# Attention values with the queries on the partitions, row sums applied after the values, and heads turned in pairs

## The chip, the core and the metric

The kernel runs on one core of a Trainium2 chip, as one launch. The metric is the time of the whole launch on the device, in microseconds (us). TensorE multiplies matrices: a weight load puts the stationary operand (up to 128x128) into the array, and a matmul streams the moving operand past it, one output row of up to 512 elements per partition, into PSUM. ScalarE (ACT), VectorE (DVE) and GpSimd (POOL) do the elementwise work, SyncE (SP) issues the transfers. The engines run side by side and wait for each other through semaphores. PE stands for TensorE's matmuls and PEld for its weight loads.

## The reference

An encoder of two layers over 512 tokens of width 1024. Each layer has an attention part with 16 heads of three kinds, an output projection, a residual with layer norm, and an MLP. The heads are 4 of kind A (a mixture of three dilated windows with a shared position bias, which the kernel folds into one softmax with a bias band), 4 of kind B (low-rank q and kv, 96 wide keys) and 8 of kind C (grouped queries on 2 key/value heads). What matters here is the core that all kinds share:

```python
def blocked_attention(q, k, v, scale):
    ...
        s = jnp.einsum('bhgqd,bhkd->bhgqk', qblk, k, preferred_element_type=jnp.float32) * scale
        p = jax.nn.softmax(s, axis=-1)
        return jnp.einsum('bhgqk,bhkd->bhgqd', p.astype(v.dtype), v)
    ...
    y = jnp.concatenate([heads_to_seq(y_a), heads_to_seq(y_b), heads_to_seq(y_c)], -1) @ w_o[l]
    x = layer_norm(ALPHA * x + (1.0 + g_a) * y, ln1_g[l], ln1_b[l])
```

Each value v is 64 wide per head, and there are 512 keys and 512 queries.

## The kernel before

Every matrix product is done in three matmuls on a split of each float32 operand into a high part of type fp32r and a low part (helper `three`, lines 1503 to 1507: high x high, high x low, low x high). ACT makes the high parts (Copy into an fp32r tile) and DVE the low ones (a subtraction).

A layer goes through the input projections, the attention, the output projection in two column halves (`wo0`, `wo1`), and eight MLP groups. Each engine has its own hand-written order for all of it, and the attention is a software pipeline over 64 units (16 heads in the order C, A, B, with 4 tiles of 128 queries each). In step s the engines do this, each in this order:

- PE (lines 1713 to 1741): the scores of unit s (stationary q of 128 queries, moving k of 512 keys, two matmuls for heads C and A, where the second half of the rows holds the low part of q, and three for B) into bank s % 3; four transposes (line 1722) of the probabilities of unit s-3 into one bank of three; and half of the values of two units. For the values the stationary operand is v (128 keys x 64) and the moving one the transposed probabilities of two units, 128 keys x 256 queries, so the output has 64 partitions (the value's elements) and 256 queries. A step has 6 of these matmuls, a head 24.
- DVE (lines 1150 to 1195): the row maximum of unit s (L1165, for heads A with the band added, L1161), the low part `pt_lo` of the transposed probabilities of unit s-4 (L1178), once per head the low part of a finished head's output (L1186, 64 partitions x 512), and the low parts of the next heads' q (L1146), k (L1139) and v (L1194).
- ACT (lines 806 to 844): Exp of unit s with the row sum (L813), the high part `pt_hi` of unit s-3 (L822), once per head the high part of a head's output (L832), and the high parts of the next q, k and v (L797, L792, L841).
- POOL (lines 529 to 542): for each unit the reciprocal of the 128 row sums (L535, a power of -1) and the scaling of the 128x512 probabilities by it (L536). In the second layer DVE takes the reciprocal for units 8 to 23 (L1172), and POOL puts behind each of these scalings one part of the layer norm's gain and shift on X (L487, L490).

PE's transposes wait for POOL's scaling (`normed`), PE's values for `pt_lo` (`pt_ready`). After the last unit PE waits for all of the low parts of the heads' output (`y_ready`), and then starts `wo0`. The heads' output goes into `hT_hi` and `hT_lo`, where the normalised activations stood before.

## Time and profile before

| | |
|---|---|
| time, median of 3 runs | 1406.24 us (1404.43 to 1406.99) |
| the profiled execution's own time | 1406.55 us |
| its span, first to last instruction | 1404.7 us |
| busy: PE, PEld, DVE, ACT, POOL | 94%, 80%, 70%, 43%, 24% |
| attention of layer 1 (l = 0): first score to first matmul of wo0 | 185.29 to 311.61 us |
| attention of layer 2 (l = 1) | 858.33 to 989.98 us |
| granted TensorE clock, mean | 0.984 of 2.4 GHz |

The busy share of PE is not a share of its peak: matmuls overlap in the trace, and what a matmul costs in a stream is the distance from its start to the next one's start. Layers are called first and second below. In a form such as `bank<-pt_hi,v_hi 128*64 128x256` the first tile is the moving operand and the second the stationary one; 128*64 is the stationary operand's shape, 128x256 the moving one's.

### The profile page before, as it was taken

To read this page: it belongs to the slowest core of one execution; us is meant where nothing else is said; L and a number is where in the kernel's file an instruction comes from. 1 tells how busy PE (TensorE), PEld (TensorE's weight loads), DVE (VectorE), ACT (ScalarE), POOL (GpSimd) and SP (SyncE) were. 2 spreads that over 40 slices of the span, in tenths; PEclk is the share of its full clock that TensorE was granted. 3 is DMA by queue.
4 is the path that set the end of the run, shared out by engine and by line. 5 is a ranking of instruction groups with operands and counts; after the bars stand their busy time and mean duration, and the time that the engine had idled before them with its cause. 6 is when DMAs were issued, how large, how long until landed. Compare 5 with 4: busy or idle time off the path is not lost.

```text
span 1404.7 us, 19902 instructions
## 1 busy us (share of the span) xinstructions
PE 1315.9 (94%) x6888; PEld 1118.5 (80%) x6888; DVE 989.6 (70%) x1676; ACT 606.0 (43%) x1260; POOL 332.1 (24%) x427
## 2 busy tenths in 40 slices
PE   4998989899999999999999899889999999999995
PEld 2888777788988888888879878678788888888884
DVE  6668789975688665755775887999377954545577
ACT  0446479871632223222254546789253222222321
POOL 0013056650324000000030404967040700000005
PEclk9999999999999999999999998999999999999998
DMA  8864500003344443442246462000225433333322
GB/s 289 301 205 147 191 27 1 28 3 111 103 151 154 155 153 95 157 156 91 83 120 235 135 217 86 1 28 1 90 68 180 154 94 98 98 97 96 98 93 95
DMA packets 88165, 164.54 MB, mean 117 GB/s; under 512 B 8024, under 2 KB 18648, under 8 KB 88080
## 3 DMA queue, kind: packets, MB, share of 16 engines
q1 hardware_dynamic: 87408, 161.08, 35.2%
q10 hardware_dynamic: 672, 2.36, 0.5%
q8 instruction: 50, 0.82, 0.2%
q14 instruction: 35, 0.29, 0.1%
HBM read 159.21 MB, written 4.19 MB: 116 GB/s over the span
## 4 chain that ended last, share of the span: by engine, by line
PE 65%; DVE 13%; DMA 7%; ACT 6%; POOL 4%; issue 3%; SPq 0%; POOLq 0%; ACTq 0%; DVEq 0%
PE bank L1505 21%; PE bank L1506 20%; PE bank L1507 20%; DMA slab_raw<-in_w_in 5%; DVE ada_sum L938 2%; PE bank L1722 2%; DVE pt_lo L1178 2%; DMA ada_w<-in_w_ada 1%; DVE smax L1165 1%; ACT slab_hi L606 1%; PE bank L1536 1%; POOL prob L536 1%; DVE q_hi L1146 1%; DVE stats L1218 1%; ACT pt_hi L822 1%
## 5 line engine op out<-in xcount | busy, mean ns | idle before, releaser
L1505 PE MATMUL bank<-hT_hi,slab_hi 128*128 128x512 f32 (+1 forms) x640 | 235.9, 369 | 2.4 <-ACT kB L755 2.4
L1506 PE MATMUL bank<-hT_lo,slab_hi 128*128 128x512 f32 (+1 forms) x640 | 235.4, 368 | 0.0
L1507 PE MATMUL bank<-hT_hi,slab_lo 128*128 128x512 f32 (+1 forms) x640 | 235.4, 368 | 0.0
L1280 DVE TENSOR_TENSOR slab_lo<-slab_raw,slab_hi 128x512 fp32r<-128x512 f32 x240 | 172.3, 769 | 66.9 <-ACT slab_hi L880 44.3
L1505 PE MATMUL bank<-slab_hi,h_hi 128*128 128x512 f32 x512 | 201.5, 394 | 0.3 <-DVE slab_lo L1280 0.3
L1507 PE MATMUL bank<-slab_hi,h_lo 128*128 128x512 f32 x512 | 199.3, 389 | 0.0
L1506 PE MATMUL bank<-slab_lo,h_hi 128*128 128x512 f32 x512 | 199.3, 389 | 0.0
L1505 PE MATMUL bank<-slab_hi,hT_hi 128*128 128x384 f32 (+3 forms) x448 | 153.8, 343 | 10.5 <-DVE slab_lo L982 4.0
L982 DVE TENSOR_TENSOR slab_lo<-slab_raw,slab_hi 128x512 fp32r<-128x512 f32 (+3 forms) x144 | 83.2, 586 | 106.2 <-ACT slab_hi L606 106.0
L498 POOL TENSOR_SCALAR mv<-mv 128x1 f32<-128x1 f32 x16 | 5.5, 345 | 642.3 <-DVE mv L1226 641.6
L1506 PE MATMUL bank<-slab_lo,hT_hi 128*128 128x384 f32 (+3 forms) x448 | 151.2, 338 | 0.0
L1507 PE MATMUL bank<-slab_hi,hT_lo 128*128 128x384 f32 (+3 forms) x448 | 151.1, 337 | 0.0
L1505 PEld LDWEIGHTS bank<-hT_hi,slab_hi 128*128 128x128 f32 x640 | 120.7, 189 | 24.0 <-ACT kB L755 4.1
L1506 PEld LDWEIGHTS bank<-hT_lo,slab_hi 128*128 128x128 f32 x640 | 120.7, 189 | 20.0
L1507 PEld LDWEIGHTS bank<-hT_hi,slab_lo 128*128 128x128 f32 x640 | 120.7, 189 | 19.9
L938 DVE SCALAR_TENSOR_TENSOR ada_sum<-ada_w,c_col,ada_sum 128x512 f32<-128x512 f32 x168 | 127.7, 760 | 12.1 <-DMA ada_w<-in_w_ada 8.2
L606 ACT ACTIVATE slab_hi<-slab_raw 128x512 fp32r<-128x512 f32 (+3 forms) x144 | 74.2, 546 | 134.9 <-DMA slab_raw<-in_w_o 73.0
L1505 PEld LDWEIGHTS bank<-slab_hi,h_hi 128*128 128x128 f32 x512 | 96.1, 188 | 21.5 <-issue 1.9
L1506 PEld LDWEIGHTS bank<-slab_lo,h_hi 128*128 128x128 f32 x512 | 96.1, 188 | 20.7 <-issue 1.0
L1507 PEld LDWEIGHTS bank<-slab_hi,h_lo 128*128 128x128 f32 x512 | 96.1, 188 | 20.1
L1313 DVE TENSOR_TENSOR acc<-bank,acc 128x512 f32<-128x512 f32 x96 | 59.6, 682 | 72.8 <-PE bank L1507 72.8
L535 POOL TENSOR_TENSOR smax<-smax,mone 128x1 f32<-128x1 f32 x112 | 70.7, 631 | 149.7 <-ACT prob L813 149.5
(199 smaller groups left out, 2565.2 us busy)
## 6 DMA issues: line engine op xcount, KB each, us to landing
slab_raw<-in_w SPq DMA_DIRECT2D x256, 256.0 KB, 2.7
ada_w<-in_w_ada SPq DMA_DIRECT2D x48, 1024.0 KB, 6.1
slab_raw<-in_w_in SPq DMA_DIRECT2D x48, 192.0 KB, 5.1
slab_raw<-in_w_o SPq DMA_DIRECT2D x32, 256.0 KB, 2.7
slab_raw<-in_w_in SPq DMA_DIRECT2D x16, 256.0 KB, 4.2
band<-bias_rows SPq DMA_DIRECT2D x8, 448.0 KB, 3.2
slab_raw<-in_w_in SPq DMA_DIRECT2D x16, 144.0 KB, 4.7
X<-in_x SPq DMA_DIRECT2D x1, 2048.0 KB, 9.6
```

What stands on the lines that cost most here:

```text
L535: after(step(pool.tensor_tensor(smax[:, u % 4, 2:3], smax[:, u % 4, 1:2], mone[:, 0:1], ALU.pow)))
L536: pool.tensor_scalar(p, p, smax[:, u % 4, 2:3], 1.0, ALU.mult, ALU.mult).then_inc(normed, 1)
L606: act.activation(slab_hi[:, slot, 0:width], slab_raw[:, slot, 0:width], ACT.Copy).then_inc(slab_hi_done, 1)
L938: return dve.scalar_tensor_tensor(out=dst, in0=ada_w[:, k // 4, k % 4, :], scalar=c_col[:, 1, k:k + 1], in1=ada_b[:, :] if k == 0 else dst ...
L982: dve.tensor_tensor(slab_lo[:, slot, 0:width], slab_raw[:, slot, 0:width], f32(slab_hi[:, slot, 0:width]), ALU.subtract).then_inc(slab_lo_ ...
L1178: dve.tensor_tensor(pt_lo[:, half % 2, :, cols], t_bank(u)[:, :].rearrange("p (k q) -> p k q", k=TT), f32(pt_hi[:, half % 2, :, cols]), AL ...
L1280: dve.tensor_tensor(slab_lo[:, slot, :], slab_raw[:, slot, :], f32(slab_hi[:, slot, :]), ALU.subtract).then_inc(slab_lo_done, 1)
L1313: dve.tensor_tensor(dst, set_[t][:, :], dst, ALU.add).then_inc(evac_dve, 1)
L1505: pe.matmul(dst, a_hi, w_hi, start=first, stop=False)
L1506: pe.matmul(dst, a_hi, w_lo, start=False, stop=False)
L1507: return pe.matmul(dst, a_lo, w_hi, start=False, stop=last)
L1722: ins = pe.transpose(t_bank(u)[:, k * P:(k + 1) * P], prob[:, u % 4, k * P:(k + 1) * P], ident[:, :])
```

## The change

The probabilities are no longer scaled. They are transposed as Exp leaves them, and in the values' product the operands change places: the transposed probabilities of one unit (128 keys x 128 queries) are the stationary operand and v (128 keys x 64) is the moving one. The output then has the queries on the partitions: 128 x 64 for each unit, 4 units side by side in one bank. When a head's four units are done, DVE multiplies its 128 x 256 output by the reciprocals of the row sums, which POOL has made for the whole head in one instruction of 4 columns. For each pair of heads PE transposes the scaled output back (4 transposes of 128x128), ACT and DVE make the high and the low part in one 128 x 512 instruction each.

The pipeline gets shorter lags (transposes 2 steps behind, low part 3, values 4). POOL's gain and shift in the second layer are spread over heads 1 to 6. For heads A the low part of k is made once in place of twice, and the second score matmul uses its 64 rows alone. The last pair's turn lies inside wo0, which starts with the parts that are ready.

```diff
-T_LAG, LO_LAG, PV_LAG = 3, 4, 6
-ATT_STEPS = UNITS + 8
-AFFINE_FROM = 8
+PAIRS = NH // 2
+T_LAG, LO_LAG, PV_LAG = 2, 3, 4
+Y_LAG = 8 + PV_LAG + 1
+ATT_STEPS = UNITS + Y_LAG - 8 + 2
+AFFINE_IN = {1: 3, 2: 3, 3: 3, 4: 3, 5: 2, 6: 2}
...
-        pt_hi = over("pt_hi", [P, 2, TT, 256], 65536, F32R)
-        pt_lo = over("pt_lo", [P, 2, TT, 256], 73728, F32R)
+        pt_hi = over("pt_hi", [P, 4, TT, P], 65536, F32R)
+        pt_lo = over("pt_lo", [P, 4, TT, P], 73728, F32R)
```

In GpSimd's program:

```diff
-                for u in range(UNITS):
-                    p = prob[:, u % 4, :]
-                    if affine_unit(l, u):
-                        pool.wait_ge(summed, sums_by_dve(l, u) + 1)
-                    else:
-                        pool.wait_ge(exped, l * UNITS + u + 1)
-                        after(step(pool.tensor_tensor(smax[:, u % 4, 2:3], smax[:, u % 4, 1:2], mone[:, 0:1], ALU.pow)))
-                    pool.tensor_scalar(p, p, smax[:, u % 4, 2:3], 1.0, ALU.mult, ALU.mult).then_inc(normed, 1)
+                def reciprocals(i):
+                    pool.wait_ge(exped, l * UNITS + 4 * i + 4)
+                    if i >= 2:
+                        pool.wait_ge(y_scaled, l * NH + i - 1)
+                    pool.tensor_tensor(rsum(i), sums(i), mone[:, 0:TT], ALU.pow).then_inc(recip_done, 1)
+                    pool.wait_ge(recip_done, l * NH + i + 1)
```

In ScalarE's:

```diff
-                        act.activation(hT_hi[64 * hf:64 * hf + 64, kt, :], bank[5 + j % 2][0:64, :], ACT.Copy
-                                       ).then_inc(y_hi_done, 1)
+                    p, off = divmod(s - Y_LAG, 8)
+                    if off == 0 and p >= 0:
+                        act.wait_ge(y_turned, l * PAIRS + p + 1)
...
+                        act.activation(hT_hi[:, kt, :], t_bank(("Y", p))[:, :], ACT.Copy).then_inc(y_hi_done, 1)
```

In VectorE's:

```diff
-                        dve.reciprocal(smax[:, u % 4, 2:3], smax[:, u % 4, 1:2]).then_inc(summed, 1)
...
+                    i, off = divmod(s - PV_LAG - TT, TT)
+                    if off == 0 and 0 <= i < NH:
+                        dve.wait_ge(pv_done, l * UNITS + 4 * i + 4)
+                        dve.wait_ge(recip_done, l * NH + i + 1)
+                        dve.tensor_tensor(y_sb(i // 2)[:, :, 64 * (i % 2):64 * (i % 2) + 64],
+                                          bank[5 + i % 2][:, 0:256].rearrange("p (t d) -> p t d", t=TT),
+                                          rsum(i).unsqueeze(2).broadcast_to([P, TT, HD]), ALU.mult
+                                          ).then_inc(y_scaled, 1)
+                    p, off = divmod(s - Y_LAG - 1, 8)
+                    if off == 0 and p >= 0:
+                        dve.wait_ge(y_hi_done, l * PAIRS + p + 1)
...
+                        dve.tensor_tensor(hT_lo[:, kt, :], t_bank(("Y", p))[:, :], f32(hT_hi[:, kt, :]),
+                                          ALU.subtract).then_inc(y_ready, 1)
```

In TensorE's:

```diff
-                        dst = bank[5 + i % 2][0:64, (half % 2) * 256:(half % 2) * 256 + 256]
-                        vs, ps = KV[i] % 2, half % 2
-                        for k in (2 * odd, 2 * odd + 1):
-                            ins = three(dst, v_hi[:, vs, k, :], v_lo[:, vs, k, :], pt_hi[:, ps, k, :], pt_lo[:, ps, k, :],
-                                        k == 0, k == TT - 1)
-                pe.wait_ge(y_ready, l * NH + NH)
-                chunk_job("wo0", WO0, 512)
+                def turn_prob(u):
+                    pe.wait_ge(exped, l * UNITS + u + 1)
+                    turn_bank_free(("P", u))
+                    for k in range(TT):
+                        ins = pe.transpose(t_bank(("P", u))[:, k * P:(k + 1) * P], prob[:, u % 4, k * P:(k + 1) * P],
+                                           ident[:, :])
+                    ins.then_inc(transposed, 1)
+                def turn_y(p):
+                    pe.wait_ge(y_scaled, l * NH + 2 * p + 2)
+                    turn_bank_free(("Y", p))
+                    for t in range(TT):
+                        ins = pe.transpose(t_bank(("Y", p))[:, t * P:(t + 1) * P], y_sb(p)[:, t, :], ident[:, :])
+                    ins.then_inc(y_turned, 1)
+                def values(u):
+                    i, qt = divmod(u, TT)
+                    pe.wait_ge(pt_ready, l * UNITS + u + 1)
+                    if qt == 0:
+                        pe.wait_ge(v_ready, l * NKV + KV[i] + 1)
+                        if i >= 2:
+                            pe.wait_ge(y_scaled, l * NH + i - 1)
+                    dst, vs = bank[5 + i % 2][:, 64 * qt:64 * qt + 64], KV[i] % 2
+                    for k in range(TT):
+                        ins = three(dst, pt_hi[:, u % 4, k, :], pt_lo[:, u % 4, k, :], v_hi[:, vs, k, :],
+                                    v_lo[:, vs, k, :], k == 0, k == TT - 1)
+                    ins.then_inc(pv_done, 1)
+                for s in range(UNITS + PV_LAG):
+                    if s < UNITS:
+                        score(s)
+                    if 0 <= s - T_LAG < UNITS:
+                        turn_prob(s - T_LAG)
+                    p, off = divmod(s - Y_LAG, 8)
+                    if off == 0 and p >= 0:
+                        turn_y(p)
+                    if 0 <= s - PV_LAG:
+                        values(s - PV_LAG)
```

The new `wo_first` does what `chunk_job("wo0", ...)` did, with `turn_y` of the last pair before its second slab, a wait for that pair's low part before its last slab, and a wait for the last head's scaling before its third token tile.

## Rows read from the trace of the kernel before

**Rows 1.** The page's first part: busy us (share of span), count, by engine.
```profile
PE 1315.9 (94%) x6888; PEld 1118.5 (80%) x6888; DVE 989.6 (70%) x1676; ACT 606.0 (43%) x1260; POOL 332.1 (24%) x427
```

**Rows 2.** Both attentions: us; busy of PE, PEld, DVE, ACT, POOL; clock, DMA share, GB/s.
```profile
185.29:311.40 126.11, 113.01 (x784) 96.59 (x784) 114.35 (x199) 107.90 (x247) 84.73 (x128) 0.99 0.03 9
858.33:989.70 131.37, 118.86 (x784) 100.91 (x784) 119.19 (x215) 108.26 (x247) 98.08 (x128) 0.94 0.03 8
```

**Rows 3.** PE's waits in the first attention: total us, times, longest us.
```profile
PE bank L1505 <- DVE pt_lo L1178: 9.0, 6, 2.2
PE bank L1722 <- POOL prob L536: 2.0, 4, 1.2
```

**Rows 4.** Timeline of PE, a unit of a C head: start us, duration us.
```profile
213.20 0.40 PE L1709 MATMUL bank<-k_hi,q_hi 128*128 128x512 f32 x1
...
213.66 0.60 PE L1722 MATMUL bank<-ident,prob 128*128 128x128 f32 x4
214.02 0.36 PE L1505 MATMUL bank<-pt_hi,v_hi 128*64 128x256 f32 x1
...
214.80 0.40 PE L1709 MATMUL bank<-k_hi,q_hi 128*128 128x512 f32 x1
```

**Rows 5.** The same for a unit of a B head, and its successor's start.
```profile
285.69 0.40 PE L1505 MATMUL bank<-k_hi,q_hi 96*128 96x512 f32 x1
...
287.52 0.40 PE L1505 MATMUL bank<-k_hi,q_hi 96*128 96x512 f32 x1
```

**Rows 6.** Timeline of PE in a projection: 128-wide weights, 256 moving columns.
```profile
136.16 0.28 PE L1505 MATMUL bank<-slab_hi,hT_hi 128*128 128x256 f32 x1
136.28 0.28 PE L1506 MATMUL bank<-slab_lo,hT_hi 128*128 128x256 f32 x1
```

**Rows 7.** Timeline of PE in the MLP: eight loads of 128 weights, one moving column each.
```profile
593.53 0.94 PE L1477 MATMUL bank<-ones,ada_sum 128*128 128x1 f32 x8
594.33 0.49 PE L1505 MATMUL bank<-slab_hi,h_hi 128*128 128x512 f32 x1
594.66 0.40 PE L1506 MATMUL bank<-slab_lo,h_hi 128*128 128x512 f32 x1
```

**Rows 8.** One line's and one tile's instructions: duration ns min/median/max.
```profile
L1477 PEld LDWEIGHTS bank<-ones,ada_sum x128: 187/192/338, 15.1 to 857.6; 128*128 128x128 f32 x128
L1505 PEld LDWEIGHTS bank<-pt_hi,v_hi x256: 132/134/231, 194.6 to 988.0; 128*64 128x64 f32 x128
```

**Rows 9.** Weight loads by form, whole span: busy us, mean ns.
```profile
L1505 PEld LDWEIGHTS bank<-hT_hi,slab_hi 128*128 128x128 f32 x640 | 120.7, 189 | 24.0 <-ACT kB L755 4.1
```

**Rows 10.** DVE's groups in the first attention: busy us, mean ns, idle before.
```profile
L1178 DVE TENSOR_TENSOR pt_lo<-bank,pt_hi 128x512 fp32r<-128x512 f32 x64 | 43.6, 684 | 2.3 <-ACT pt_hi L822 1.1
L1186 DVE TENSOR_TENSOR hT_lo<-bank,hT_hi 64x512 fp32r<-64x512 f32 x16 | 10.9, 679 | 1.9 <-ACT hT_hi L832 1.7
L1139 DVE TENSOR_TENSOR k_lo<-qkA,k_hi 64x512 fp32r<-64x512 f32 x8 | 5.5, 687 | 1.7 <-ACT k_hi L792 1.5
L1194 DVE TENSOR_TENSOR v_lo<-vA,v_hi 128x256 fp32r<-128x256 f32 x4 | 1.7, 417 | 0.1
```

**Rows 11.** POOL's scalings in the second attention: busy us, mean ns.
```profile
L536 POOL TENSOR_SCALAR prob<-prob,smax 128x512 f32<-128x512 f32 x64 | 46.7, 729 | 5.5 <-DVE smax L1172 0.8
```

**Rows 12.** Timeline of PE, end of the first attention: idle us before, its releaser.
```profile
311.61 0.50 PE L1505 MATMUL bank<-slab_hi,hT_hi 128*128 128x512 f32 x1 [1.40 <-DVE hT_lo L1186]
```

**Rows 13.** Windows of 1 us, granted clock in the third column from the end.
```profile
188.00:189.00 1.00, 0.90 (x3) 0.30 (x2) 0.28 (x2) 0.95 (x4) 0.71 (x2) 0.90 0.00 0
867.00:868.00 1.00, 1.00 (x7) 0.87 (x6) 1.00 (x2) 1.00 (x3) 0.90 (x3) 0.77 0.00 0
925.00:926.00 1.00, 1.00 (x7) 0.94 (x6) 0.97 (x2) 0.48 (x1) 0.83 (x2) 0.74 0.00 0
```

**Rows 14.** Timeline of PE ahead of the last of those windows.
```profile
924.80 0.33 PE L1505 MATMUL bank<-pt_hi,v_hi 128*64 128x256 f32 x1 [1.84 <-DVE pt_lo L1178]
```

**Rows 15.** The chain that ended last, a stretch at half clock: start us, us.
```profile
41.54 1.88 PE bank L1477 x8
```

More of the change, by code:

```diff
@@ L81, with turns @@
 UNITS = NH * TT
-T_LAG, LO_LAG, PV_LAG = 3, 4, 6
-ATT_STEPS = UNITS + 8
-AFFINE_FROM = 8
-def affine_unit(l, u):
-    return l > 0 and AFFINE_FROM <= u < AFFINE_FROM + 4 * TT
-def sums_by_dve(l, u):
-    return sum(affine_unit(m, v) for m in range(l) for v in range(UNITS)) + sum(affine_unit(l, v) for v in range(u))
+PAIRS = NH // 2
[3 more added lines that the diff above has]
+AFFINE_IN = {1: 3, 2: 3, 3: 3, 4: 3, 5: 2, 6: 2}
+def turns():
+    out = []
+    for s in range(ATT_STEPS):
+        if 0 <= s - T_LAG < UNITS:
+            out.append(("P", s - T_LAG))
+        if s >= Y_LAG and (s - Y_LAG) % 8 == 0:
+            out.append(("Y", (s - Y_LAG) // 8))
+    return out
+TURNS = turns()
+TURN = {job: n for n, job in enumerate(TURNS)}
 OUT_AT = [(4 + h // 2, h % 2) if m == "C" else (h // 2, h % 2) if m == "A" else (2 + h // 2, h % 2)
@@ L528, in _ @@
                     pool.sem_inc(x_ready, TT)
-                for u in range(UNITS):
-                    p = prob[:, u % 4, :]
-                    if affine_unit(l, u):
-                        pool.wait_ge(summed, sums_by_dve(l, u) + 1)
-                    else:
-                        pool.wait_ge(exped, l * UNITS + u + 1)
-                        after(step(pool.tensor_tensor(smax[:, u % 4, 2:3], smax[:, u % 4, 1:2], mone[:, 0:1], ALU.pow)))
-                    pool.tensor_scalar(p, p, smax[:, u % 4, 2:3], 1.0, ALU.mult, ALU.mult).then_inc(normed, 1)
-                    if l > 0 and u == AFFINE_FROM:
-                        pool.wait_ge(bank_ready, l * B_LAYER + 16)
-                        pool.wait_ge(lnx_in, 32)
-                    if affine_unit(l, u):
-                        n = u - AFFINE_FROM
-                        affine_part(n // 4, n % 4, lnx_g, lnx_b)
+                def reciprocals(i):
[4 more added lines that the diff above has]
+                    pool.wait_ge(recip_done, l * NH + i + 1)
+                part = 0
+                for i in range(NH):
+                    if i >= 1:
+                        reciprocals(i - 1)
+                    for _ in range(AFFINE_IN.get(i, 0) if l > 0 else 0):
+                        if part == 0:
+                            pool.wait_ge(bank_ready, l * B_LAYER + 16)
+                            pool.wait_ge(lnx_in, 32)
+                        affine_part(part // 4, part % 4, lnx_g, lnx_b)
+                        part += 1
+                        if part % 4:
+                            after(steps[0])
+                        else:
+                            pool.wait_ge(x_ready, l * 8 + part // 4)
+                reciprocals(NH - 1)
                 normalise(0)
@@ L1708, in score, with turn_bank_free @@
                     else:
+                        at = head_q(i)[2] if m == "A" else slice(0, P)
                         pe.matmul(dst, q_hi[:, s, q], k_hi[:, ks, :], start=True, stop=False)
-                        ins = pe.matmul(dst, q_hi[:, s, q], k_lo[:, ks, :], start=False, stop=True)
+                        ins = pe.matmul(dst, q_hi[at, s, q], k_lo[at, ks, :], start=False, stop=True)
                     ins.then_inc(scored, 1)
-                for s in range(ATT_STEPS):
+                def turn_bank_free(job):
+                    n = TURN[job] - 3
+                    if n >= 0:
+                        kind, x = TURNS[n]
+                        if kind == "P":
+                            pe.wait_ge(pt_ready, l * UNITS + x + 1)
+                        else:
+                            pe.wait_ge(y_ready, l * PAIRS + x + 1)
@@ L1743, in _, with wo_first @@
-                pe.wait_ge(y_ready, l * NH + NH)
-                chunk_job("wo0", WO0, 512)
+                    if 0 <= s - T_LAG < UNITS:
+                        turn_prob(s - T_LAG)
[4 more added lines that the diff above has]
+                        values(s - PV_LAG)
+                def wo_first():
+                    free_after("wo0")
+                    pe.wait_ge(y_ready, l * PAIRS + PAIRS - 1)
+                    for k in range(8):
+                        kt = WO_ORDER[k]
+                        if k == 1:
+                            turn_y(PAIRS - 1)
+                        if k == 7:
+                            pe.wait_ge(y_ready, l * PAIRS + PAIRS)
+                        slab_ready(l * SLABS + 8 * WO0 + k + 1)
+                        for t in range(TT):
+                            if k == 0 and t == 2:
+                                pe.wait_ge(y_scaled, l * NH + NH)
+                            ins = three(banks(JOB["wo0"])[t][:, :], hT_hi[:, kt, t * P:(t + 1) * P],
+                                        hT_lo[:, kt, t * P:(t + 1) * P], slab_hi[:, k, :], slab_lo[:, k, :],
+                                        k == 0, k == 7)
+                        ins.then_inc(slab_free, 1)
```

120 lines of the change are left out of this document (46 added, 74 removed).

## The prediction

> **What bounds the kernel now.** The page's first part says that PE is busy 94% of the span [rows 1], but such a share says little where matmuls overlap, so the next view is the windows, cut to the two attentions, which are all that the change touches. There PE is busy 113.0 of 126.1 us and DVE 114.4 in the first, 118.9 and 119.2 of 131.4 in the second [rows 2]: two engines near their limit, ACT not far behind. PE's waits show the balance: 9.0 us for `pt_lo`, 2.0 us for POOL's scaling [rows 3]. The timeline of PE then gives what a unit costs it when nothing is late. I read the distances between starts, not the durations. For a head C or A: two score matmuls 213.20 to 213.66 = 0.46 us, four transposes and their turnover to the next unit's values; a whole unit is 213.20 to 214.80 = 1.60 us [rows 4]. A transpose costs 0.110 (four in 0.60, less the 0.27 that one takes, is 0.33 for three), so four cost 0.44, and 0.70 is left for the six values' matmuls, 0.117 each. A B head's unit is 285.69 to 287.52 = 1.83 [rows 5], for its third score matmul. Over 48 and 16 units that is 48 x 1.60 + 16 x 1.83 = 106.1 us. From the first score to wo0 it took 126.3 us (185.29 to 311.61) in the first layer and 131.7 (858.33 to 989.98) in the second, so 20 and 26 us were waits, the start, the end, and stretches at the lower clock. Those are the most that the change can win.
>
> **The values' product, the large term.** Before, a unit has 6 matmuls with 64-wide weights and 256 moving columns. After, it has 12, with 128-wide weights and 64 moving columns. The moving columns fall from 1536 to 768, the columns of weights rise from 384 to 1536. No row shows a 128-wide fp32r load followed by 64 columns, so I bound it:
> - From below by the moving side alone. 512 columns cost 0.23 [rows 4] and 256 cost 0.12 [rows 6], so 64 would cost 0.04 if the load hid.
> - By the load. Eight loads of 128 with a single moving column each begin at 593.53, and the next matmul begins at 594.33; it lasts 0.49 instead of 0.40, so it really began 0.09 later [rows 7]. That is 0.80 to 0.89 for eight, 0.10 to 0.11 each, with nothing but the load to pay for. At half clock eight take 1.88 with a last one of about 0.37, so 0.216 each [rows 15]: it goes by the array's clock.
> - Does an fp32r load cost what these float32 loads cost? Their shown durations are alike, 189 against 187 to 192 ns, while a 64-wide load shows 134 [rows 8, 9]. 55 ns more for 64 more columns would be 110 for 128.
> - 128-wide fp32r weights with 256 moving columns come every 0.12 [rows 6], so a load takes at most that beside a running matmul.
> - From above, if a load can't hide under so short a matmul: 0.110 + 0.04 = 0.15.
>
> I take 0.111, because rows 7 and the step in rows 8 and 9 agree on it and each isolates the load; 0.107 to 0.12 is the near range. Twelve cost 1.33 where six cost 0.70. The Trainium skill, page "TensorE: Matmul & The Clock Gate", section on LDWEIGHTS, puts a load at its columns divided by 1.2 GHz, 107 ns for 128, and its table on weight-path modes leaves float32 out of the fast load; the trace agrees at about 0.11.
>
> **PE's sum.** A unit C or A after: 0.46 + 0.44 + 1.33 = 2.23. The eight turns of pairs add 4 x 0.11 each, 0.44 x 8 / 64 = 0.055 a unit: 2.29. A B head's unit adds 0.23: 2.52. 48 x 2.29 + 16 x 2.52 = 150.2 us per layer, against 106.1.
>
> **What DVE, ACT and POOL get back.** DVE in the first layer: 114.4, less 16 low parts of the output at 0.679 (10.9), plus 8 at the same length though they have 128 partitions (5.4), plus 16 scalings of 128x256, not in the trace, nearest `v_lo` with the same shape at 0.417 (6.7; between that and 0.68, the length of a 512 wide instruction, 10.9), less 4 second low parts of k at 0.687 (2.7): 112.9 (to 117), and 2.5 less in the second layer for the reciprocals [rows 10]. ACT makes 8 output parts less. POOL loses 64 scalings of 0.729 [rows 11] and most powers, and with them one link of about 1.3 us in each unit's chain; it keeps one power per head, and in the second layer three parts of gain and shift behind it, hidden by the 9 us of the head that follows, since the scaling asks for that power only a step after the head's last values. Against a PE of 150 us none of it is on the path. For a head of kind A, the heaviest, DVE needs 4 x (0.68 + 0.08 + 0.68) + 0.69 + 0.69 + 0.42 + 0.42 + 0.34 = 8.3 us and PE 4 x 2.29 = 9.2: DVE becomes the second, and PE's waits on `pt_lo` (9.0 us) shrink to what the order leaves, taken as 2 us. The new waits of DVE (for the values of a head finished one step before, and for POOL's power) stand behind the step's maximum and low part, so the next maximum is what queues behind them; PE asks for the scaled output of head i only at the values of head i+2.
>
> **Start and end.** The start stays: 1.2 GHz until about 188 [rows 13] costs 1.5 us, the first trips through the engines 2.5. In the second layer the lower clock lasted from 858 to 867.8 [rows 13]; POOL's link is gone, PE works sooner without gaps, and I put clock and first trips at 5. At the end PE waited 1.40 us for the last output's low part [rows 12]; now the last pair is turned inside wo0, and this wait goes.
>
> **The sum.** First layer 150.2 + 4 + 2 = 156.2 against 126.3: +29.9. Second layer 150.2 + 5 + 2 = 157.2 against 131.7: +25.5. Together +55.4 on the profiled execution's 1406.55, 1462 us; the median of the runs, 1406.24, is the same within 0.03%.
>
> **Rivals.**
> 1. Slower by more, the load doesn't hide: 0.15 each adds 0.039 x 1536 = 60 us: 1522. Rows 6 speak against it, since there the load lies beside a matmul; but that one is four times as long.
> 2. Faster: the loads hide. The place is PE's values; the mechanism is that fp32r weights are taken faster than float32 ones and the shown 189 ns is latency. With y us per matmul the two layers cost 2 x (48 x 0.955 + 16 x 1.185) + 13 + 1536 y = 142.6 + 1536 y, against 258.0 before, so it decides at y = 0.075. At 0.04 PE's unit is 1.44 and DVE binds: its 112.9 of work at the same share of busy time as now gives about 124.5 for the first layer, less the 1.4 at the end; the second comes down to the same: 1406.55 - 3 - 8 = 1395. For it: DVE is as busy as PE now, and POOL's waits go. Against it: rows 7, 8 and 9.
> 3. Partly hidden, y near 0.08: 265.5 us for the two layers, 1414. A middle between bounds, borne out by no row of its own. The same page of the Trainium skill gives a stream of load and matmul pairs at 128 moving columns 81 ns per matmul; no row here shows 81 ns, and transposes of 128 columns come every 110.
> 4. The clock is lost. It was at 1.2 GHz when both attentions began, behind a run of single-column matmuls, and again from 925.7 on, after PE had idled 1.84 us [rows 13, 14]; it came back while long matmuls ran. In the changed unit PE moves few columns between loads, so it might not come back. A unit would cost about twice 2.29. Half of the units of both layers: 64 x 2.3 = 147 us, 1609; all: some 1750. Against it: PE has hardly any gaps after the change.
>
> **Chances.** The forecast (1450 to 1482) 66%; rival 1 6%; rival 2 13%; rival 3 8%; rival 4 7%. The range takes in forecast, rivals 1 and 3 and what touches them: 1403 to 1525. The forecast's own: 0.107 gives -6, 0.12 gives +14, and waits of 0 to 5 us per layer instead of 2 give -4 to +6, so 1450 to 1482. By 0.2% (2.8 us, about what a measurement of this kernel can tell from no change), faster is 12% (nearly all of rival 2), the same 4%, slower 84%.
>
> **What the changed profile would show.** The starts of the values' matmuls in one unit 0.11 apart, twelve in 1.33 us; if 0.15, rival 1; if 0.04, rival 2. A unit's period of 2.3 us for C, 2.5 for B, with PE's waits on `pt_lo` at a few us per layer, and DVE's busy share in the attention down from 91% to about 72%. The attentions 156 us long each. No wait before wo0. POOL below 35 us in the first attention's stretch. A granted clock below 0.9 in the attention would show rival 4. The prediction is wrong if the distance of the values' matmuls is not between 0.10 and 0.12, or if PE's waits exceed 10 us per layer, since then another engine sets the pace.

## The result and the profile after

| | before | after |
|---|---|---|
| time, median | 1405.87 us (5 runs, 1404.43 to 1406.99) | 1600.32 us (5 runs, 1586.14 to 1630.72) |
| ratio after to before, 95% interval | | 1.1322 (1.1295 to 1.135) |
| the profiled execution's own time | 1406.55 us | 1630.72 us |
| its span | 1404.7 us | 1628.8 us |
| first attention, first score to wo0 | 126.3 us | 204.8 us (185.8 to 390.6) |
| second attention | 131.7 us | 271.9 us (939.2 to 1211.2) |

The change makes the kernel 13% slower, where 4% was forecast and the range ended at 1525. The ratio is taken over the executions within 1.5% of their kernel's fastest, which are three of the five after; the medians in the table stand 14% apart. The executions of the changed kernel differ by up to 45 us, those of the kernel before by 3. The profiled one is the longest of the five, and what differs between them is how long TensorE's clock stayed low: the mean granted clock goes from 0.909 in the shortest to 0.884 in the longest.

The page of the changed kernel, the parts that answer to [rows 1, 2]: busy time by engine, and the rows of PE and of the granted clock over 40 slices of the span.

```profile
PE 1563.8 (96%) x7720; PEld 1347.9 (83%) x7720; DVE 983.4 (60%) x1668; ACT 599.9 (37%) x1244; POOL 203.1 (12%) x219
...
PE   5989999999999999999998999999999999999996
...
PEclk9999997569999999999999985555559999999998
```

PE is busy for 96%, DVE's work has hardly changed (983 us against 990), POOL has lost 129 us. In the clock's row stands what the busy shares hide: about half speed in slices 7 to 9 and from the end of slice 24 to slice 30 (a slice is 40.7 us), which lie in the attentions.

The timeline of PE, a unit of a C head at full clock, which answers to [rows 4] (start us, duration us):

```profile
239.74 0.48 PE L1735 MATMUL bank<-k_hi,q_hi 128*128 128x512 f32 x1
240.05 0.39 PE L1736 MATMUL bank<-k_lo,q_hi 128*128 128x512 f32 x1
240.28 0.60 PE L1754 MATMUL bank<-ident,prob 128*128 128x128 f32 x4
240.63 0.28 PE L1530 MATMUL bank<-v_hi,pt_hi 128*128 128x64 f32 x1
240.75 0.28 PE L1531 MATMUL bank<-v_lo,pt_hi 128*128 128x64 f32 x1
240.86 0.28 PE L1532 MATMUL bank<-v_hi,pt_lo 128*128 128x64 f32 x1
...
241.86 0.28 PE L1532 MATMUL bank<-v_hi,pt_lo 128*128 128x64 f32 x1
241.97 0.48 PE L1735 MATMUL bank<-k_hi,q_hi 128*128 128x512 f32 x1
```

The values' twelve matmuls begin at 240.63 and the next score at 241.97: 1.34 us, 0.112 each. The unit takes 241.97 - 239.74 = 2.23 us. Both are the numbers of the forecast. Inside the rest of the unit two of its terms are off and cancel: the two scores take 0.54 us in place of 0.46, the transposes 0.35 in place of 0.44.

The same view where the heads of kind A begin:

```profile
255.87 0.48 PE L1735 MATMUL bank<-k_hi,q_hi 128*128 128x512 f32 x1
256.28 0.50 PE L1736 MATMUL bank<-k_lo,q_hi 64*128 64x512 f32 x1
256.71 0.66 PE L1754 MATMUL bank<-ident,prob 128*128 128x128 f32 x4
...
258.47 0.48 PE L1735 MATMUL bank<-k_hi,q_hi 128*128 128x512 f32 x1
```

Here a unit takes 2.60 us, 0.37 more than the C unit above. The score matmul that uses 64 rows begins 0.41 after its predecessor (0.31 in the C head), and what follows it begins 0.43 later (0.23). Going from 128 rows to 64 and back costs time, and this part of the change had no term in the sum.

Windows of 1 us where the clock falls in the first attention (first two lines) and in the second; columns as in [rows 2], the clock is third from the end:

```profile
259.00:260.00 1.00, 1.00 (x8) 0.75 (x8) 0.76 (x2) 0.63 (x1) 0.00 (x0) 1.00 0.00 0
260.00:261.00 1.00, 1.00 (x10) 1.00 (x9) 0.97 (x4) 0.85 (x3) 0.00 (x0) 0.85 0.00 0
...
969.00:970.00 1.00, 1.00 (x11) 1.00 (x11) 0.97 (x2) 0.81 (x2) 0.00 (x0) 1.00 0.00 0
970.00:971.00 1.00, 1.00 (x9) 1.00 (x9) 1.00 (x3) 0.78 (x3) 0.00 (x0) 0.84 0.00 0
```

In the first attention PE had no gap ahead of the fall: every window of 1 us from 193 on shows it busy for 1.00. In the second it had idled 0.62 us, waiting for Exp, about 1.8 us before the fall:

```profile
968.90 0.63 PE L1754 MATMUL bank<-ident,prob 128*128 128x128 f32 x4 [0.62 <-ACT prob L846]
```

In the kernel before, the clock fell in mid-attention behind waits of 1.84 us [rows 14] and 2.17 us (at 942.6), and came back within 4 us both times. Now it stayed at 1.2 GHz from 260.7 to 356.3, and from 970.7 to 1216.4, where wo0 had begun with its 512 column matmuls. In these stretches the values' matmuls come twice as far apart, 0.21 us (299.63 to 300.27 for three), as the same view shows:

```profile
299.63 0.40 PE L1530 MATMUL bank<-v_hi,pt_hi 128*128 128x64 f32 x1
299.85 0.40 PE L1531 MATMUL bank<-v_lo,pt_hi 128*128 128x64 f32 x1
300.06 0.40 PE L1532 MATMUL bank<-v_hi,pt_lo 128*128 128x64 f32 x1
```

PE waits for others only 1.4 us in the whole first attention, so it sets the pace, and about half of the time at half clock is lost: (95.6 + 245.7) / 2 = 170.7 us, an estimate from these stretches. 1630.7 less 170.7 is 1460.0. The forecast had 1462; how near that is owes something to luck, since two errors in it partly cancel (see PE's sum below).

### The profile page after: what moved, and what is told of

The parts are those of the page before. It is cut to its first block, busy times and chain, and to the rows that moved or that the text cites. A ratio compares the mean times of both kernels' runs of the same rounds, so it can differ in the third digit from the quotient of the medians.

```text
span 1628.8 us, 21434 instructions
## 1 busy us (share of the span) xinstructions
PE 1563.8 (96%) x7720; PEld 1347.9 (83%) x7720; DVE 983.4 (60%) x1668; ACT 599.9 (37%) x1244; POOL 203.1 (12%) x219
## 4 chain that ended last, share of the span: by engine, by line
PE 80%; DVE 7%; DMA 6%; ACT 3%; POOL 2%; issue 1%; SPq 0%; POOLq 0%; ACTq 0%; DVEq 0%
PE bank L1531 23%; PE bank L1532 23%; PE bank L1530 22%; PE bank L1754 5%; DMA slab_raw<-in_w_in 4%; PE bank L1735 2%; PE bank L1736 2%; DVE ada_sum L969 1%; DMA ada_w<-in_w_ada 1%; PE bank L1561 1%; ACT slab_hi L643 1%; DVE stats L1243 1%; DVE sqr L1226 1%; PE bank L1763 1%; DVE slab_lo L1013 1%
## 5 line engine op out<-in xcount | busy, mean ns | idle before, releaser
L1530 PE MATMUL bank<-v_hi,pt_hi 128*128 128x64 f32 x512 | 178.5, 349 | 1.1 <-DVE pt_lo L1195 1.1
L1532 PE MATMUL bank<-v_hi,pt_lo 128*128 128x64 f32 x512 | 178.5, 349 | 0.0
L1531 PE MATMUL bank<-v_lo,pt_hi 128*128 128x64 f32 x512 | 178.4, 348 | 0.0
L1190 DVE TENSOR_REDUCE smax<-bank 128x1 f32<-128x512 f32 x96 | 66.3, 691 | 141.8 <-PE bank L1532 75.7
L1530 PEld LDWEIGHTS bank<-v_hi,pt_hi 128*128 128x128 f32 x512 | 140.0, 274 | 1.6 <-DVE pt_lo L1195 1.6
L1532 PEld LDWEIGHTS bank<-v_hi,pt_lo 128*128 128x128 f32 x512 | 139.9, 273 | 0.0
L1531 PEld LDWEIGHTS bank<-v_lo,pt_hi 128*128 128x128 f32 x512 | 139.9, 273 | 0.0
```

Of the source, the lines that this page charges most:

```text
L1190: dve.tensor_reduce(smax[:, s % 4, 0:1], bank[s % 3][:, :], AX.X, ALU.max, negate=True).then_inc(maxed, 1)
L1530: pe.matmul(dst, a_hi, w_hi, start=first, stop=False)
L1531: pe.matmul(dst, a_hi, w_lo, start=False, stop=False)
L1532: return pe.matmul(dst, a_lo, w_hi, start=False, stop=last)
```

## The experiments

Times are medians with the range of the executions. A ratio is against the kernel before on the same chip, whose median was 1405.8 to 1406.5 us. e1 to e4 ran on one chip, e5 to e8 on a second and e9 to e12 on a third; the changed kernel itself was not run again beside them, so a difference from its 1600 us can hold something of the chip. Each run has one profiled execution.

**e1, all rows in the A heads' scores.**

```diff
-            return KV[i] % 2, ksrc, both, both if m == "C" else both[:1]
+            return KV[i] % 2, ksrc, both, both
...
-                        at = head_q(i)[2] if m == "A" else slice(0, P)
+                        at = slice(0, P)
```

> The changed kernel, with one part undone: heads of kind A use all 128 rows in their second score matmul again, and the low part of k is made in both halves. In the changed kernel's trace a unit of an A head takes 2.60 us against 2.24 of a C head, though it has the same matmuls but for these 64 rows, and the clock fell to half at the first A head in one layer. Theory 1 (the clock goes for lack of moving columns between the many weight loads, whatever the rows): the A unit comes down to 2.24 (12 us less in both layers at full clock), but the clock still falls in the attention and the time stays within 1560 to 1615. Rival (the 64-row matmuls bring the clock down): the granted clock stays at full in the attention and the time is about 1462.

1499.42 us (1461.69 to 1511.11). A unit of an A head lasts from 263.38 to 265.63, 2.25 us, as theory 1 had it. But neither forecast of the clock came true. The clock's row of the page:

```profile
PEclk9999999999999999999999997559999999999998
```

The first attention is now at full clock until 337.7, just before its end. In the second the clock is low from 921.4 to 1020.4, which lies among heads C and A, all of them on 128 rows here; this fall too came behind a wait of 0.62 us for Exp. One execution of four held the clock nearly throughout (mean 0.987): that one took 1461.69. The median is 101 us under the changed kernel's, of which some 11 us are the shorter A units, so the 64-row matmuls do bring the kernel nearer to the fall, but the clock also falls without them. The expectation of 1560 to 1615 was wrong.

**e2, more moving columns under the same loads.**

```diff
-                    dst, vs = bank[5 + i % 2][:, 64 * qt:64 * qt + 64], KV[i] % 2
+                    vs = KV[i] % 2
                     for k in range(TT):
+                        n = 2 if k < TT - 1 else 1
+                        dst = bank[5 + i % 2][:, 128 * qt:128 * qt + 64 * n]
                         ins = three(dst, pt_hi[:, u % 4, k, :], pt_lo[:, u % 4, k, :],
-                                    v_hi[:, vs, k, :], v_lo[:, vs, k, :], k == 0, k == TT - 1)
+                                    v_hi[:, vs, k:k + n, :].rearrange("p k d -> p (k d)"),
+                                    v_lo[:, vs, k:k + n, :].rearrange("p k d -> p (k d)"), k == 0, k == TT - 1)
```

> The changed kernel, with 9 of a unit's 12 values' matmuls moving 128 columns in place of 64; the second 64 go to columns of the bank that nobody reads. The same number of loads and matmuls, more moving columns. Theory 1 (load-paced, and the clock falls because too few columns move): the distance of these matmuls stays at 0.11 us, the clock holds, and the time falls to what the work costs at full clock: 2 x (32 x 2.24 + 16 x 2.60 + 16 x 2.48 + 3.5 + 6) = 325 us for the two attentions against 258 before, 1473. Rival A (the distance is set by the moving columns at a slower rate for short matmuls): it doubles to about 0.22 for the wide ones, a unit takes 3.2 us, and the time is 1600 or more. Rival B (the clock falls for another reason): distance 0.11, clock still at half for long stretches, time 1580 to 1630.

1465.56 us (1463.68 to 1467.89), ratio 1.0419 (1.039 to 1.0448). The clock's row and a stretch of PE's timeline:

```profile
PEclk9999999999999999999999999999999999999998
```

```profile
241.17 0.27 PE L1532 MATMUL bank<-v_hi,pt_lo 128*128 128x128 f32 x1
241.28 0.27 PE L1530 MATMUL bank<-v_hi,pt_hi 128*128 128x128 f32 x1
241.40 0.28 PE L1531 MATMUL bank<-v_lo,pt_hi 128*128 128x128 f32 x1
```

The distance stays at 0.11 us with twice the columns, so it is the load's. The clock holds (mean 0.989 in all four executions), the spread shrinks from 45 to 4 us, and 135 us are gone, though the kernel only does more. Of the three outcomes expected this is theory 1's, 7 us below its number. PE's wait of 0.62 us for Exp in the second attention is still there, at 921.32, and the clock does not fall behind it. The A heads still have their 64-row matmuls. So neither that wait nor those matmuls bring the clock down when more columns move. The two attentions take 158.5 and 159.8 us.

**e6, fewer moving columns under the same loads.** The two low products move 32 columns; the corrections of the other 32 value columns are left out.

```diff
-                        ins = three(dst, pt_hi[:, u % 4, k, :], pt_lo[:, u % 4, k, :], v_hi[:, vs, k, :],
-                                    v_lo[:, vs, k, :], k == 0, k == TT - 1)
+                        pe.matmul(dst, pt_hi[:, u % 4, k, :], v_hi[:, vs, k, :], start=k == 0, stop=False)
+                        pe.matmul(dst[:, 0:32], pt_hi[:, u % 4, k, :], v_lo[:, vs, k, 0:32], start=False, stop=False)
+                        ins = pe.matmul(dst[:, 0:32], pt_lo[:, u % 4, k, :], v_hi[:, vs, k, 0:32], start=False,
+                                        stop=k == TT - 1)
```

> The opposite of e2: in the changed kernel the two low products of the values move 32 columns in place of 64 (the corrections of the other 32 value columns are left out). Loads and their number stay. Theory (load-paced; the clock falls for lack of moving columns): the distance stays 0.11 us at full clock and 0.22 at half, no time is won by moving less, and the clock is at half in more of the attention than in the changed kernel: 1620 to 1750. Rival (moving columns cost time in such short matmuls): faster than the changed kernel's 1586 to 1631.

1665.91 us (1658.32 to 1673.5), ratio 1.1843 (1.1787 to 1.19). The clock's row, and PE's timeline at full clock:

```profile
PEclk9999995555999999999999965555559999999998
```

```profile
240.44 0.28 PE L1776 MATMUL bank<-v_hi,pt_hi 128*128 128x64 f32 x1
240.55 0.26 PE L1777 MATMUL bank<-v_lo,pt_hi 128*128 128x32 f32 x1
240.66 0.26 PE L1778 MATMUL bank<-v_hi,pt_lo 128*128 128x32 f32 x1
240.77 0.28 PE L1776 MATMUL bank<-v_hi,pt_hi 128*128 128x64 f32 x1
```

32 columns cost what 64 and 128 cost, 0.11 us, and less work made the kernel 66 us slower; there are only two executions, but both lie above all five of the changed kernel. The clock was low from 255.8 to 423.1 and from 982.9 to 1259.3, 444 us against 341 in the changed kernel's profile. The first fall came 2.4 us after the first A head's score, the second among the C heads, with no gap on PE for 8 us before it. From 32 over 64 to 128 columns the time goes 1666, 1600, 1466, with the same number of loads.

**e5, e1 and e2 together.** Its diff is the two above. Against e1 it differs in the moving columns alone.

> The two edits of e1 and e2 together: 128 moving columns in 9 of 12 values' matmuls, and all 128 rows in the second score matmul of heads A. e2 gave 1465.6 us with the clock at full throughout. In e2's trace a unit of an A head takes 2.59 us, in e1's 2.25; 0.35 x 16 units x 2 layers = 11 us. Theory: 1454, clock at full; what is left against the kernel before is the price of the loads alone. Rival (the 64-row matmuls cost nothing at the end, since DVE, which has to make the second low part of k again, sets the pace of the A heads): 1463 or more.

1458.12 us (1454.4 to 1458.43), ratio 1.0357 (1.0335 to 1.038): 7 us of the 11 expected against e2, on another chip. In the profiles the two attentions take 153.0 and 154.3 us, together 11.0 less than e2's, as expected. The clock holds, and again it does not fall behind the wait for Exp, behind which it fell in e1 for 99 us:

```profile
917.26 0.63 PE L1754 MATMUL bank<-ident,prob 128*128 128x128 f32 x4 [0.62 <-ACT prob L846]
```

What is left is the price of the loads, less what the waits give back. The values' product costs 12 x 0.112 - 0.70 = 0.64 us a unit more, times 128 units, 82 us, and the turned pairs add 7. Against that, start, end and waits, the part of both attentions that is not in PE's sum, fell from 46 us to 7. That makes 50 us; measured are 49 in the attentions and 52 in the time. PE's waits in its first attention:

```profile
PE bank L1530 <- DVE pt_lo L1195: 0.6, 1, 0.6
PE bank L1735 <- DVE q_hi L1171: 0.4, 1, 0.4
```

against 9.0 and 2.0 before [rows 3].

**e4, the values' product cut to high x high,** 4 matmuls in place of 12 (the low products are left out).

```diff
-                        ins = three(dst, pt_hi[:, u % 4, k, :], pt_lo[:, u % 4, k, :], v_hi[:, vs, k, :],
-                                    v_lo[:, vs, k, :], k == 0, k == TT - 1)
+                        ins = pe.matmul(dst, pt_hi[:, u % 4, k, :], v_hi[:, vs, k, :], start=k == 0, stop=k == TT - 1)
```

> The changed kernel, with the values' product reduced to high x high: 4 matmuls a unit in place of 12 (the two products with low parts are left out). What is left of the change is the unscaled probabilities, the scaling afterwards and the turned pairs. Theory 1: PE's unit is 1.35 us for C, DVE sets the pace with about 124 us per layer, and the clock holds, since the columns that remain come close together: about 1396 to 1405. Rival (the rest of the change costs time as well, by the new waits for the scaled output and the turned pairs): above 1415.

1397.07 us (1393.86 to 1422.15), ratio 0.9929 (0.9898 to 0.996). With 4 loads a unit for the values the kernel gains 9 us: this is about what rival 2 had been worth (1395). In the first attention, now 117.4 us long, DVE is busy for 109.6, and 6.6 of PE's 9 us of waits there are for DVE's `pt_lo`. Two of five executions, at 1419 and 1422, had a mean clock of 0.96 against 0.98 in the others, so the clock was lost for longer there. The expectation that it holds came true only in part: in the profiled execution, the shortest, its mean is 0.92 in the second attention.

**e3, high and low part of v side by side,** so that each high part of the probabilities is loaded once: 8 loads a unit.

```diff
-                        ins = three(dst, pt_hi[:, u % 4, k, :], pt_lo[:, u % 4, k, :], v_hi[:, vs, k, :],
-                                    v_lo[:, vs, k, :], k == 0, k == TT - 1)
+                        pe.matmul(dst, pt_hi[:, u % 4, k, :], v_both[:, vs, k, :], start=k == 0, stop=False)
+                        ins = pe.matmul(dst[:, 0:64], pt_lo[:, u % 4, k, :], v_both[:, vs, k, 0:HD], start=False,
+                                        stop=k == TT - 1)
...
+                        step(dve.tensor_copy(ysum, both[:, :, HD:2 * HD]))
+                        settle()
+                        step(dve.tensor_tensor(ysum, both[:, :, 0:HD], ysum, ALU.add))
```

> The changed kernel with the high and the low part of v side by side as one moving operand of 128 columns, so that the transposed probabilities' high part is loaded once in place of twice: 8 loads a unit in place of 12, the same columns moved. DVE adds the two halves of the output, two more instructions of 128x256 per head. Theory 1 (load-paced at 0.11): a unit loses 0.44 us, the C unit goes to 1.80, and with more columns in less time the clock holds: 2 x (32 x 1.80 + 16 x 2.16 + 16 x 2.04 + 3.5 + 10) = 277, so 1425, with DVE close behind PE. If the clock falls nonetheless, 1500 or more. Rival (column-paced): a unit's values cost as before the edit and the time stays above 1460.

1447.8 us (1430.72 to 1516.62). The lowest execution is 6 us above the sum, the others lost the clock for longer or shorter (mean 0.984 down to 0.922), so the forecast of the clock was wrong again: the same columns in less time did not hold it.

**e9, e3 with 128 moving columns in both matmuls and all rows in the A heads' scores.**

```diff
-                        ins = pe.matmul(dst[:, 0:64], pt_lo[:, u % 4, k, :], v_both[:, vs, k, 0:HD], start=False,
-                                        stop=k == TT - 1)
+                        ins = pe.matmul(dst, pt_lo[:, u % 4, k, :], v_both[:, vs, k, :], start=False, stop=k == TT - 1)
```

> e3 (high and low part of v side by side, 8 loads a unit) with 128 moving columns in both of its matmuls and all 128 rows in the second score matmul of heads A. e3 ran from 1430.7 to 1516.6 with the clock falling in some executions. Theory (few moving columns bring the clock down; the loads cost 0.11 each): the executions lie within 5 us of each other, and the time is e5's 1458 less 4 loads a unit (4 x 0.11 x 128 = 57 us), plus what DVE's two more instructions a head (0.42 each) add where DVE sets the pace: 1405 to 1425. Rival (the clock falls nonetheless): a spread of over 15 us.

1436.28 us (1435.54 to 1440.06), ratio 1.022 (1.02 to 1.0241). The spread is 4.5 us, as expected; the time is 11 us above the expectation. Windows over its attentions (the first a little wider than the attention) and PE's waits in the first:

```profile
185.00:325.00 140.00, 130.76 (x947) 113.98 (x948) 125.99 (x238) 104.08 (x238) 16.17 (x16) 0.99 0.03 8
871.42:1019.56 148.14, 135.82 (x940) 119.30 (x941) 129.55 (x235) 104.21 (x238) 37.61 (x32) 0.94 0.02 7
```

```profile
PE bank L1780 <- DVE pt_lo L1195: 4.2, 4, 1.5
PE bank L1767 <- DVE tmp L1208: 2.3, 7, 0.4
PE bank L1758 <- DVE pt_lo L1195: 1.4, 2, 0.7
PE bank L1758 <- ACT prob L846: 1.2, 2, 0.8
```

DVE is busy 126 of 140 us, 90%, its share in the kernel before, and PE waits for it again: of the 57 us of saved loads 22 arrive. In the second attention the clock fell three times after its start, for 3.4, 3.4 and 6.8 us, each time behind a wait of PE of 1.4 to 2.8 us. So with 128 columns the clock can still fall behind a wait, but it comes back by itself within 7 us, where it stayed low for 99 us in e1. Even so, and with a third of the loads gone, this orientation stays behind the kernel before.

**The rest of the change, taken back to the kernel before.** e7: the A heads' second score matmul on 64 rows, the low part of k made once.

```diff
-                    for at, to in parts:
+                    for at, to in (parts[:1] if HEADS[i][0] == "A" else parts):
...
+                        at = head_q(i)[2] if m == "A" else slice(0, P)
-                        ins = pe.matmul(dst, q_hi[:, s, q], k_lo[:, ks, :], start=False, stop=True)
+                        ins = pe.matmul(dst, q_hi[at, s, q], k_lo[at, ks, :], start=False, stop=True)
```

> The kernel before with one part of the change alone: heads of kind A use 64 rows in the second score matmul and DVE makes that low part of k once. PE's unit of an A head would grow by 0.35 us to 1.95, still under what DVE needs there (2.2 us before, about 2.05 with one instruction of 0.69 less per head). Theory (DVE sets the pace in the A heads): 4 x 0.69 x 2 = 5.5 us of DVE less, 2 to 5 us won: 1401 to 1404. Rival (PE, through the longer units and the order, sets it): no change or up to 6 us slower.

1401.75 us (1400.76 to 1403.17), ratio 0.9963 (0.995 to 0.9976). PE's waits in the first attention:

```profile
PE bank L1505 <- DVE pt_lo L1178: 2.9, 5, 1.2
PE bank L1505 <- DVE hT_lo L1186: 1.4, 1, 1.4
```

The units of the A heads cost PE 0.34 us more (250.02 to 251.96 is 1.94), and its waits on `pt_lo` fall from 9.0 to 2.9 us: the same edit that costs 7 to 11 us where PE is the bound (e2 against e5: 7 in the medians, 11 in the attentions) wins 4 to 5 where DVE is.

e8: wo0 starts with the slabs that are ready, and POOL's parts are spread.

```diff
-AFFINE_FROM = 8
+AFFINE_FROM, AFFINE_STEP = 6, 3
...
-                pe.wait_ge(y_ready, l * NH + NH)
-                chunk_job("wo0", WO0, 512)
+                pe.wait_ge(y_ready, l * NH + NH - 2)
+                free_after("wo0")
+                for k in range(8):
...
+                        if k == 0 and t == 2:
+                            pe.wait_ge(y_ready, l * NH + NH)
```

> The kernel before with two side parts of the change carried over, the values' product untouched: wo0 begins with the slabs whose heads are ready and waits for the last head only at its third token tile, and the 16 gain and shift parts of POOL in the second layer stand at every third unit from 6 on in place of every unit from 8 to 23. Theory: the wait of 1.4 us before wo0 goes in both layers (2.8 us), and of the 5 us by which the second attention was longer than the first 2 to 4 go: about 1400. Rival (PE waits for the slabs or for DVE anyway): within 1 us of before.

1404.7 us (1401.9 to 1405.55), ratio 0.9988 (0.9977 to 0.9999). Less than expected: the wait of [rows 12] is gone, but in the second layer PE's waits on `pt_lo` grew:

```profile
PE bank L1505 <- DVE pt_lo L1178: 10.6, 8, 3.1
```

from 7.1 us in the kernel before.

> The kernel before with e7's edit and the earlier start of wo0 from e8, without the spread of gain and shift. e7 gave 1401.75, e8 1404.7 with the wait of 1.4 us gone in both layers. Theory (the two add up): 1401.75 - 2.8 = 1399. Rival (the wait before wo0 was won back by something behind it): 1401 to 1402.

e11 (the diffs of e7 and e8 without the spread): 1396.4 us (1395.1 to 1397.77), ratio 0.9934 (0.9919 to 0.9948). It beats both kernels.

> e11 with the spread of the gain and shift parts as well. e8's trace shows PE's waits on the low part of the probabilities in the second layer grown from 7.1 to 10.6 us with the spread. Theory (the spread keeps POOL's parts beside DVE's work for longer and is worth nothing or costs): the same as e11 within 1.5 us. Rival (the spread is worth what POOL's full stretch cost): 2 to 4 us less than e11.

e12 (with the spread): 1397.48 us (1395.92 to 1401.83), ratio 0.9946 (0.9929 to 0.9963). The spread is worth nothing.

**e10, the kernel before with no scaling at all.** The division by the row sums is left out.

```diff
-                        after(step(pool.tensor_tensor(smax[:, u % 4, 2:3], smax[:, u % 4, 1:2], mone[:, 0:1], ALU.pow)))
-                    pool.tensor_scalar(p, p, smax[:, u % 4, 2:3], 1.0, ALU.mult, ALU.mult).then_inc(normed, 1)
...
-                        pe.wait_ge(normed, l * UNITS + u + 1)
+                        pe.wait_ge(exped, l * UNITS + u + 1)
```

> The kernel before with the scaling of the probabilities left out and nothing in its place (the output is not divided by the row sums); the values' product keeps its old operands. It isolates what unscaled probabilities can give. Theory (DVE sets the pace of the attention, POOL's scaling is mostly hidden): 3 to 8 us, 1398 to 1403, most of it in the second layer, where POOL also has the gain and shift. Rival (the scaling's 1.3 us in each unit's chain matter): 12 us or more, under 1394.

1400.92 us (1398.8 to 1405.53), ratio 0.9966 (0.9953 to 0.9978). PE's waits in the first attention:

```profile
PE bank L1495 <- DVE pt_lo L1168: 7.6, 6, 2.2
PE bank L1495 <- DVE hT_lo L1176: 1.4, 1, 1.4
```

The scaling on POOL, which the change removes, was worth about 5 us (3 to 7 by the interval). In the profiles the first attention keeps its length, 126.0 us against 126.3, so there the scaling was hidden behind DVE. All of the gain is in the second, 126.0 against 131.7. There POOL also had the gain and shift, but the clock differs too: around the second attention it was low for 17 us in the kernel before and for 3.4 in this profile. How much of the 5 us is the scaling's stays open.

## Why the prediction was wrong, point by point

- **What bounds the kernel.** Right: DVE and PE together. e7 shows DVE's part: with 4 low parts of k a layer gone it won 4 us, though PE's units got longer. e10 shows that POOL's 64 scalings a layer were worth little, about 5 us.
- **The values' product.** Right, and the rows that isolate the load gave the number: 0.111 taken, 0.112 measured, the same at 32, 64 and 128 moving columns (e6, e2). One reading was wrong and cost nothing: [rows 15] was taken as a stretch at half clock, while the granted clock shows 1.00 from 41 to 44 us (its first lower value comes at about 120), so that the loads there were slow for the clock is not shown by that row. That a load's distance goes by the clock is shown by the changed kernel, 0.21 us at a granted 0.50 against 0.112. Rivals 1, 2 and 3 fall with the measured distance; e4 shows that rival 2's time would have been nearly right if the product had been cheap.
- **PE's sum.** A C unit at full clock is 2.23 as computed. Missing is a term: the A heads' 64-row matmul costs 0.35 us a unit, 0.35 x 32 = 11 us, which came off e5's attentions to the full and 7 us off its time; the edit was noted as half the k work of DVE and costed at nothing on PE. No row before showed it, and it should have been bounded. Start, waits and end were taken as 13 us for both layers and came out at about 7 (e2's 318.3 us of attention, less 2 x 150.2 and the 11). The two errors partly cancel, and so the full-clock time came out at 1465.6 in e2 against 1462: that it is so near is partly luck.
- **DVE, ACT, POOL.** Right: PE hardly waits any more (1.0 us in e5's first attention against 2 taken), DVE has slack (busy for 114 of 153 us there).
- **The clock.** This is the step that failed: the sum took every unit at full clock, and TensorE's clock was at 1.2 GHz for 341 us of the profiled execution, with a mean of 0.75 of full speed in the first attention and 0.55 in the second. That is the sign which the prediction had named for rival 4. Rival 4 had the step, with its place and its price (1609 for half of the units; the median is 1600), and got 7% on the argument that PE has hardly any gaps after the change. The argument reads the wrong thing. In the first attention the clock fell with PE busy in every window ahead of it, and of three kernels with the same loads the one that moves 128 columns kept the clock and the one that moves 32 lost it for longest (e2, e6). The trace of the kernel before had a sign of it. Ahead of both attentions 32 loads with one moving column each follow each other; ahead of the second the clock fell inside that run, at 857.2, with PE busy for 1.00 of every microsecond from 848 on:

```profile
854.10 3.97 PE L1477 MATMUL bank<-ones,ada_sum 128*128 128x1 f32 x32
...
857.00:858.00 1.00, 1.00 (x7) 0.98 (x6) 1.00 (x2) 0.04 (x1) 0.00 (x0) 0.61 0.00 0
```

  The forecast cited the run and still argued from gaps. The Trainium skill, page "TensorE: Matmul & The Clock Gate", Part 1, puts the clock down to how busy PE has been recently and warns of idle gaps. Here PE's busy share was 1.00 over the windows in which the clock fell, so the trace doesn't agree with a reading by idle gaps or by the profile's busy share, and the measurement decides.
- **The range.** It ended at 1525, since rival 4 was left outside with its 7%. A case with a price of 150 us and more on one side wants a better reason than one sentence before it is left out.

Shown is that the loss of the clock makes the difference to the forecast, and that it goes away with more moving columns and grows with fewer, under the same loads. Not settled is what exactly brings the clock down and why it falls where it does. It fell in the second A unit in one layer and among the C heads in the other. Only one execution was profiled, and the times of the five, 1586 to 1631, say that the stretches were not equally long in all. e1 and e3 have executions with a short and with a long loss for one and the same kernel. The changed kernel stands near an edge, and the runs don't say where the edge is.

## What to carry to other kernels

Count weight columns as well as moving columns when operands change places: a product that moves half the columns but loads four times as many weight columns costs the load, 0.11 us for each 128 wide fp32r load as long as 128 columns or fewer move with it. In a stream of such short matmuls TensorE's clock fell to half while PE was busy all the time, so look for stretches at lower clock behind small matmuls in the trace, and price the loss at twice PE's work. Where the loads set the pace, moving more columns under each load, even useless ones, was free and kept the clock. If an engine is one of two near-equal bounds, take the side edits of a change back one by one: here two small ones alone gave 0.66% (e11), while the whole change cost 13%.

## What the runs showed of the hardware

- More moving columns under the same loads made the kernel faster: 1666, 1600 and 1466 us for 32, 64 and 128 columns in most of the values' matmuls. The distance was 0.11 us for each at full clock; for 64 columns it was 0.21 us at 1.2 GHz.
- The same wait of 0.62 us on PE was followed by a fall of the clock for 246 us in the changed kernel and for 99 us in e1, and by no fall in e2 and e5, where 128 columns move. In e9, also with 128 columns, three falls behind longer waits were over within 7 us.
- In the changed kernel the clock stayed at 1.2 GHz for 96 and 246 us; it came back in a B head in one case, and 5 us after wo0's 512-column matmuls had begun in the other. In e1 it came back in an A head.
- A matmul on 64 rows between matmuls on 128 rows costs PE about 0.35 us in all in this stream (2.60 against 2.25 us a unit after, 1.94 against 1.60 in the kernel before), though it moves the same columns.
- The first 512-column score matmul behind the row of 64-column ones is followed by the next one 0.31 us later (239.74 to 240.05); in the kernel before, behind 256-column ones, it was 0.23 (half of the 0.46 in [rows 4]).
